# A four-layer decoder step on eight cores: tile-contiguous buffers, chained first loads, cast loads in order of use, and pooling by one 144-column band matmul

## The reference, cut to what matters

```python
def pool_mixer(h, buf, start_pos, w_pool, scale):      # layers 1 and 3, windows 2, 4, 8, 16
    ...
    p = (mean - hc[:, L:]).astype(h.dtype).reshape(B, T, N_POOL_GROUPS, GD_B)
    y = jnp.einsum('btgc,gce->btge', p, w_pool).reshape(B, T, D)
    return y * scale, hc[:, -L:].astype(h.dtype)

def trunk(x, ...):
    for i in range(DEPTH):
        h = rmsnorm(x, norm_mix[i])
        y = gmlp_mixer(h, ...) if i % 2 == 0 else pool_mixer(h, ...)
        x = x + y
        h = rmsnorm(x, norm_ffn[i])
        y, cb = conv_ffn(h, ...)          # silu(conv(h @ w_gate)) * (h @ w_val) @ w_down
        x = x + y
    return rmsnorm(x, norm_final), ...
```

## Time and profile before

| | us |
|---|---|
| median of 3 runs | 2949.17 (2947.11 to 3199.98) |
| the profiled execution | 2947.15 |
| its span (core 3; the cores lie between 2922.9 and 2945.6) | 2945.6 |

### The profile page before, as it was taken

The page is one execution under the profiler, slowest core; times in us unless marked ns, Lnnn a source line. Parts: engine busy times, 40 slices in busy tenths (PEclk is TensorE's granted clock), DMA queues, the critical chain, the costliest instruction groups (busy, mean ns, idle before and its releaser), DMA issues.

```text
span 2945.6 us, 52581 instructions; the slowest of 8 cores (2922.9 to 2945.6 us)
## 1 busy us (share of the span) xinstructions
PE 2812.8 (95%) x18576; PEld 1778.1 (60%) x18576; DVE 1489.3 (51%) x3134; ACT 1235.1 (42%) x2385; POOL 469.8 (16%) x832
## 2 busy tenths in 40 slices
PE   1999999999999999999987999999999999999998
PEld 0545666666654666666654566665766566666665
DVE  1266662565217566266531556626642366625753
ACT  1543443544244344354325434436433435435531
POOL 1002221132200222213220020020011020010001
PEclk9999999899999999999998999998999999998999
DMA  9516341554253543135444453322544335314421
GB/s 171 109 31 115 59 78 29 95 94 86 48 95 53 101 73 71 37 78 97 88 97 101 74 109 72 73 37 51 91 90 72 72 71 97 62 32 85 85 54 58
DMA packets 55425, 227.84 MB, mean 77 GB/s; under 512 B 6240, under 2 KB 25312, under 8 KB 37600
## 3 DMA queue, kind: packets, MB, share of 16 engines
q0 software_dynamic: 32960, 193.75, 37.4%
q1 hardware_dynamic: 22208, 30.72, 3.3%
HBM read 406.32 MB, written 13.32 MB: 142 GB/s over the span
## 4 chain that ended last, share of the span: by engine, by line
PE 87%; DMA 4%; DVE 3%; issue 3%; ACT 2%; DVEq 0%; SPq 0%; ACTq 0%
PE psum L720 27%; PE psum L989 22%; PE psum L982 21%; PE psum L786 8%; PE psum L809 4%; DMA xT<-x_in 4%; PE psum L945 2%; PE psum L649 1%; PE psum L897 1%; DVE vn_47 L823 1%; DVE vn_48 L823 0%; PE psum L841 0%; DVE nwt L743 0%; DMA gmlp_v<-gout 0%; DVE nwt L744 0%
## 5 line engine op out<-in xcount | busy, mean ns | idle before, releaser
L723 DVE TENSOR_TENSOR xT<-psum,xT 128x384 f32<-128x384 f32 (+2 forms) x288 | 148.0, 522 | 497.7 <-PE psum L720 482.2
L1006 DVE SCALAR_TENSOR_TENSOR cb_96<-psum,pvf,cb_96 128x384 f32<-128x384 f32 (+1 forms) x264 | 150.8, 571 | 70.3 <-ACT cb_96 L996 57.8
L1006 DVE SCALAR_TENSOR_TENSOR cb_97<-psum,pvf,cb_97 128x384 f32<-128x384 f32 (+1 forms) x264 | 150.7, 571 | 51.1 <-ACT cb_97 L996 31.0
L1006 DVE SCALAR_TENSOR_TENSOR cb_99<-psum,pvf,cb_99 128x384 f32<-128x384 f32 (+1 forms) x264 | 150.7, 571 | 48.9 <-ACT cb_99 L996 26.7
L1006 DVE SCALAR_TENSOR_TENSOR cb_98<-psum,pvf,cb_98 128x384 f32<-128x384 f32 (+1 forms) x264 | 150.6, 571 | 46.2 <-ACT cb_98 L996 32.9
L621 ACT ACTIVATE sq_59<-xT 128x384 f32<-128x384 f32 (+2 forms) x126 | 61.8, 491 | 191.0 <-DVE xT L723 174.0
L621 ACT ACTIVATE sq_60<-xT 128x384 f32<-128x384 f32 (+2 forms) x126 | 61.8, 491 | 171.7 <-DVE xT L723 155.6
L727 ACT ACTIVATE hB<-xT,pvd 128x384 bf16<-128x384 f32 (+1 forms) x96 | 55.4, 577 | 186.7 <-DVE xT L723 168.3
L996 ACT ACTIVATE cb_99<-psum,pvf 128x384 f32<-128x384 f32 (+2 forms) x132 | 84.4, 639 | 104.0 <-PE psum L982 103.8
L996 ACT ACTIVATE cb_96<-psum,pvf 128x384 f32<-128x384 f32 (+2 forms) x132 | 84.5, 640 | 99.3 <-PE psum L982 97.4
L672 DVE SCALAR_TENSOR_TENSOR hB<-xT,pvd,rstd_66 128x384 bf16<-128x384 f32 (+2 forms) x192 | 101.5, 600 | 45.6 <-ACT rstd_66 L664 41.4
(11 more groups left out here) (818 smaller groups left out, 6395.9 us busy)
## 6 DMA issues: line engine op xcount, KB each, us to landing
xT<-x_in SPq DMA_DIRECT2D x8, 768.0 KB, 19.8
y_out<-mT SPq DMA_DIRECT2D x8, 768.0 KB, 4.6
ASb<-st_conv SPq DMA_DIRECT2D x4, 1056.0 KB, 9.3
gvb<-g_v SPq DMA_DIRECT2D x4, 1024.0 KB, 8.2
pool_old<-st_old SPq DMA_DIRECT2D x2, 704.0 KB, 6.7
conv_sample<-cst SPq DMA_DIRECT2D x4, 352.0 KB, 6.3
xT<-x_in SPq DMA_DIRECT2D x2, 640.0 KB, 7.2
y_out<-mT SPq DMA_DIRECT2D x2, 640.0 KB, 6.3
```

Source lines behind the costliest of these rows:

```text
L723: rec(DVE, lambda e: e.tensor_tensor(out=xT.t[:, dc, c0:c0 + n], in0=pap(bk, 0, n), in1=xT.t[:, dc, c0:c0 + n], op=ALU.add), pt=[(bk, Fals ...
L1006: rec(DVE, lambda e: e.scalar_tensor_tensor(out=cb.t[:, 0:npr], in0=pap(gb, 2 - sh, 2 - sh + npr), scalar=sc(3 * l + 2 - sh), in1=cb.t[:, ...
```

## The change

- x, `mT` and `UB` get one buffer per tile, [128, blocks, n], so that a tile's rows follow each other without a gap in each partition; the z tiles, `vn` and `hS` move into parts of these buffers, and the final output has its own view of `mT` with whole rows.
- First loads: `pvd` first, then x tile 0; `Uu` 0 in two halves behind the first half of x tile 0; x tile 1 behind the first half of `Uu` 0; `Uu` 1 in two halves behind tile 1's first half; x tile 2 behind the first half of `Uu` 1; `Uu` 2 behind tile 2's first half. The very first u unit of tile 0 runs block of 128 input channels by block, over four PSUM banks, so that it can begin with the first normalised block. The Ln table is loaded by a small activation ahead.
- Each DMA of SP and POOL is ordered behind the one recorded before it in the same queue (`order`, for the planner alone, with no semaphore wait). The planner adds 0.5 us to the start of an operation that would change the ACT table when it compares candidates.
- Pooling: `band` gets 144 columns per group; one matmul over all 128 partitions writes a chunk's 128 columns and the first 16 of the next chunk. The chunk before a tile gives its 16 columns in one matmul of its own over 128 partitions. `bprev` is gone. Only the first matmul of a bank has `start`.
- Seam: `first_norm` of the next group's tile 0 comes after tile 1's load, those of tiles 1 and 2 after tile 2's load; its squares are added on DVE. The last tile of the run sums squares on PE, and its store goes in four parts.

```diff
@@ rec, schedule, emit
+        for o in order:
+            deps.setdefault(o, None)
...
-                if bs is None or s < bs - 1e-9:
+                k = s if op.tab is None or op.tab == lasttab[name] else s + 0.5
+                if bs is None or k < bk - 1e-9:
...
+                if u.deps[op] is None:
+                    u.ready = max(u.ready, op.start + op.cost)
...
@@ buffers
-        xT = alloc("xT", [128, KC, NTMAX], F32, pieces=grid(KC, NTMAX))
+        xv = {(g, t): alloc(f"xT{g}{t}", [128, KC, TILES[g][t][1]], F32, off=XO + sum(NT[:t]) * KC * 4, ...
...
+                mv[(g, t)] = alloc(f"mT{g}{t}", [128, FC, n], BF16, off=MO[t], ...
+                ubv[(g, t)] = alloc(f"UB{g}{t}", [128, EC, n], BF16, off=MO[t], ...
+                yv[(g, t)] = alloc(f"yT{g}{t}", [128, KC, n], F32, off=MO[t], ...
...
+        zb = [zalloc(f"z{c}", MO[0] + 6144 + 2048 * c) for c in range(3)]
+        zb += [zalloc(f"z{c}", MO[1] + o) for c, o in ((3, 0), (4, 2048), (5, 6144), (6, 8192), (7, 10240))]
...
@@ dma
+            op = rec(eng, lambda e: e.dma_start(out=out, in_=in_), reads, writes, cost, dsem, nbytes, behind=behind, order=fifo[eng.name][-1:])
+            fifo[eng.name].append(op)
...
@@ first loads
+        const_load(pvd, pvd.t[:, :, :].rearrange("p a b -> p (a b)"), vec_d, SP)
         xl0 = load_x(0, 0)
-        load_unit(("Uu", 0, 0, 0), behind=xl0[:1])
-        xl1 = load_x(0, 1, behind=xl0[1:])
-        load_unit(("Uu", 0, 0, 1))
-        xl2 = load_x(0, 2, behind=xl1[1:])
-        load_unit(("Uu", 0, 0, 2))
-        load_unit(("Uu", 0, 0, 3))
+        u0 = load_unit(("Uu", 0, 0, 0), behind=xl0[:1], parts=2)
+        xl1 = load_x(0, 1, behind=[u0.op0])
+        u1 = load_unit(("Uu", 0, 0, 1), behind=xl1[:1], parts=2)
+        xl2 = load_x(0, 2, behind=[u1.op0])
+        u2 = load_unit(("Uu", 0, 0, 2), behind=xl2[:1])
+        u3 = load_unit(("Uu", 0, 0, 3))
...
+        rec(ACT, lambda e: e.activation(out=rstd[1].t[:, 0:1], in_=epsb.t[:, 0:1], func=AF.Ln), ...
...
@@ mixer_a, first u unit of tile 0
+                    if (g, l, u, t) == (0, 0, 0, 0):
+                        b4 = palloc(4)
+                        for kc in range(KC):
+                            def mmu4(e):
+                                for e4 in range(4):
+                                    i = e.matmul(pap(b4, e4 * 512, e4 * 512 + n), lhsT=ub.t[:, kc, e4 * 128:(e4 + 1) * 128], ...
...
@@ mixer_b_tile
-                        else:
+                        if c == cl[0] and not (g == 0 and c == 0):
                             zp = zprev if c == 0 else ztile[c - 1]
-                            lst.append(((oc, oc + 128), zt.t[:, zh, es_], band.t[:, gi, :], True))
-                            lst.append(((oc, oc + 16), zp.t[96:128, zh, es_], bprev.t[96:128, gi, :], False))
+                            lst.append(((0, 16), zp.t[:, zh, es_], band.t[:, gi, 128:144]))
+                        tail = 0 if c == cl[-1] else 16
+                        if g == 0 and c == 0:
+                            lst.append(((0, 128), zt.t[:, zh, es_], bhi.t[:, gi, :]))
+                            lst.append(((0, 128), zt.t[:, zh, es_], blo.t[:, gi, :]))
+                            lst.append(((128, 144), zt.t[:, zh, es_], band.t[:, gi, 128:144]))
+                        else:
+                            lst.append(((oc, oc + 128 + tail), zt.t[:, zh, es_], band.t[:, gi, 0:128 + tail]))
...
@@ first_norm, final_tile, after_ffn
+                if lead:
+                    stat_add_pe(g, t, kc, DVE if kc % 2 else ACT)
+                else:
+                    stat_add(g, t, kc, DVE)
...
+            np_ = 4 if g == NG - 1 and t == 2 else 2
...
                             load_x(g + 1, t)
-                            first_norm(g + 1, t)
+                            if t > 0:
+                                first_norm(g + 1, t - 1)
+                            if t == 2:
+                                first_norm(g + 1, t)
```

More of the change, by code:

```diff
@@ L121, in __init__, with rec @@
         self.ops = []
-    def rec(self, eng, fn, reads=(), writes=(), cost=0.0, dsem=None, nbytes=0, tab=None, pt=(), behind=()):
+    def rec(self, eng, fn, reads=(), writes=(), cost=0.0, dsem=None, nbytes=0, tab=None, pt=(), behind=(), order=()):
         op = Op()
@@ L558, in build_program, with load_unit @@
         loaded = {}
-        def load_unit(key, behind=()):
+        def load_unit(key, behind=(), parts=1):
             i = unit_index[key]
             _, src, a, b, off, nb = units[i]
-            buf = alloc(f"w{i}", [128, a, b], BF16, off=R0 + off)
+            buf = alloc(f"w{i}", [128, a, b], BF16, off=R0 + off, pieces=[(h, h * a * b // parts, (h + 1) * a * b // parts) for h in range(parts)])
             so = src_off[src]
             sap = wts[so:so + 128 * a * b].rearrange("(p c) -> p c", p=128)
-            dma(POOL, buf.t[:, :, :].rearrange("p a b -> p (a b)"), sap, writes=buf.all, dsem=ring_sems[i % NRS], nbytes=128 * a * b * 4, behind=behind)
+            for h in range(parts):
+                cs_ = slice(h * a * b // parts, (h + 1) * a * b // parts)
+                buf.op = dma(POOL, buf.t[:, :, :].rearrange("p a b -> p (a b)")[:, cs_], sap[:, cs_], writes=[buf.r[h]], dsem=ring_sems[(i + 8 * h) % NRS],
+                             nbytes=128 * a * b * 4 // parts, behind=behind)
+                buf.op0 = buf.op0 if h else buf.op
+                behind = ()
             loaded[key] = buf
@@ L636, in stat_add @@
             d = a if kc < KC - 1 else accb[t % 2]
-            eng = POOL if kc < KC - 1 else DVE
+            eng = aeng or (POOL if kc < KC - 1 else DVE)
             rec(eng, lambda e: e.tensor_tensor(out=d.t[:, 0:n], in0=a.t[:, 0:n], in1=s.t[:, 0:n], op=ALU.add),
@@ L757, in mixer_a @@
             if first:
-                const_load(maskT, maskT.t[:], c_mask, behind=xl2[1:])
-            dma(SP, gvb.t[:], g_v[j].partition_broadcast(128), writes=gvb.all, dsem=gv_sem, nbytes=1048576, behind=xl2[1:] if first else ())
+                const_load(maskT, maskT.t[:], c_mask)
+            dma(SP, gvb.t[:], g_v[j].partition_broadcast(128), writes=gvb.all, dsem=gv_sem, nbytes=1048576, behind=[u3.op] if first else ())
             dma(POOL, wsT.t[:, :, :].rearrange("p a b -> p (a b)"), w_sT[j], writes=wsT.all, dsem=ws_sems[0], nbytes=524288)
@@ L1031, in mm_list @@
                 c0, n = TILES[g][t]
-                return ([(w.t[:, fc, :], mT.t[:, fc, c0:c0 + n]) for fc in range(FC)], w.all + [mT.r[(fc, t)] for fc in range(FC)])
+                return ([(w.t[:, fc, :], mv[(g, t)].t[:, fc, :]) for fc in range(FC)], w.all + [mv[(g, t)].r[fc] for fc in range(FC)])
             for t in range(3):
-                proj_tile(g, t, mm_list, l + 1 if l % 2 == 0 else None)
+                proj_tile(g, t, mm_list, l + 1 if l % 2 == 0 else None, l == DEPTH - 1)
                 after_tile(t)
         def first_norm(g, t):
+            lead = (g, t) == (0, 0)
             for kc in range(KC):
-                stat_add_pe(g, t, kc, DVE if (g == 0 and kc % 2) else ACT)
-            stat_finish(g, t, pe=True)
+                if lead:
+                    stat_add_pe(g, t, kc, DVE if kc % 2 else ACT)
+                else:
+                    stat_add(g, t, kc, DVE)
+            stat_finish(g, t, pe=lead)
             norm_tile(g, t, 0)
@@ L1169, in make_in_maps @@
     f = lambda k: np.asarray(inputs[k], dtype=np.float32)
-    mask, band, bhi, blo, bprev, bsmp = _consts()
+    mask, band, bhi, blo, bsmp = _consts()
     vd = np.concatenate([f("norm_mix"), f("norm_ffn"), f("norm_final").reshape(1, D), f("scale_b"), np.zeros((1, D), np.float32)], 0)
@@ L1185, in make_in_maps @@
         "w_sT": wsT, "w_sm": wsm.reshape(2, 64, 512), "b_big": np.ascontiguousarray(b_big), "b_smp": b_smp,
-        "c_mask": mask, "c_band": band, "c_bhi": bhi, "c_blo": blo, "c_bprev": bprev, "c_bsmp": bsmp,
+        "c_mask": mask, "c_band": band, "c_bhi": bhi, "c_blo": blo, "c_bsmp": bsmp,
     }
```

180 lines of the change are left out of this document (95 added, 85 removed).

## The result

The kernel after takes 2827.3 us (2825.5 to 2827.3), and 0.9591 of the time before, 95% interval 0.9569 to 0.9613. In some executions the cores of one die or of both run at a lower granted clock and take some per cent longer; all times and ratios here leave these out. Differences in us are against this 2827.3. The forecast of 2828 came out within 1 us. Its terms did not: two were too large, one too small, and they cancelled.

What follows compares the result with a forecast made beforehand. The prediction took PE's stream of matmuls as the bound. Gains of 46 (head), 47 (pooling), 25 (seam) and 1.5 (tail) sum to 119.5 us, giving 2828 us, with an 8-in-10 range of 2793 to 2874.

Steps and rivals of the forecast that it cites:

- Head: Start of the kernel: x and u units land earlier, v's first matmul at 84 instead of 129.95 us, gain 46.
- rival 4: DMA queues: a load that waits holds later ones, PE waits at 16 sub-layers, up to 3020 us; chance 0.03.
- Pooling: Four pooling stretches: 45 us from cheaper band pairs, 6 lost to new waits, 8 gained from the clock; gain 47.
- the sign of 5: Pooling: PE waiting for ACT or DVE for more than 5 us a stretch would show the prediction wrong.
- ACT is not the bound: 0: Whole kernel: fewer table changes save ACT time, but ACT is not the bound, so gain 0.
- Seam: Between the two groups: longer transfer rows, a sum by one matmul and earlier u work of tile 0; gain 25.
- Tail: End of the kernel: last sum off POOL and DVE, last store a quarter, less 0.5 for 8 matmuls; gain 1.5.
- 1: Pooling becomes bound by DVE and ACT and gives 12 us instead of 47: 2863 us; chance 0.15.
- 2: Head and seam: load chains are slow and the seam stays DMA-bound, gains 30 and 8: 2861 us; chance 0.13.
- 3: All gains plus full clock without new waits in pooling, and a head at 80: 2800 us; chance 0.17.
- Rival 5: Pooling: the band matmul stays at 0.15 us because of the write into the same bank, 2848 us; chance 0.07.
- The rule of the Trainium skill: Pooling: by the issue-gap formula a pair costs 81 ns and the change saves 1 us, 2872 us; chance 0.02.

Runs made afterwards that it cites:

- b_one: The kernel after, with the four bias rows loaded by one DMA and the two bias rows of the samples by another: 2822.1 us, ratio 0.9570.
- p_two_full: The kernel after, with each pooling pair as two matmuls of 128 and 16 columns, both over all 128 partitions: 2826.7 us, ratio 0.9585.
- the two pair runs: The kernel after, with each pooling pair as two matmuls, the second over all 128 partitions (2826.7 us) or over the last 32 as before (2875.3 us).

## Why the prediction was right in its sum and wrong in its terms

- **What bounds the kernel**: right. Idle PE time, wasted PE time and low clock were the three places, and all three gave.
- **Head, 46 forecast, 36.1 measured.** PE started at 16.6 for 15.5, steady u at 33.0 for 30, u ended at 89.8 for 84: each near, 6 late in the end, with waits for u units of 3.5 and 3.2. The step that failed is "the v units need 4.2 MB more ... about 80, in time". They landed until 98, and PE waited 4.9 for the last, because the four bias loads, counted there as "small constants", each waited for a landing and held the queue. That is rival 4's mechanism at one place; b_one takes 7.4 us of it back. "PE waiting for a weight unit anywhere" was one of the signs of being wrong, and it came. The reason given for the gain, that nothing competes with x's tile 0, was half right: the order of the loads keeps competitors away (without it the head is 26 us longer, 30.5 in the mean), the new links on top of it are worth 3 to 6. "Loads in order of use: 0" was thus wrong in the other direction.
- **Pooling, 47 forecast, 66.5 measured.** The 45 for the pairs held, and p_two_full confirmed its reason. The two corrections were both too small and cancelled: clock 14 for 8 (a remainder), new waits 13 for 6. The reason for the waits was off, too: in the first stretch PE waits 1.8 us for ACT's evictions of z (L937), and 0.7 for DVE's residual adds (L988). With 3.6 to 5.3 us of idle PE a stretch, two of the four are just above the sign of 5. What was missing is the ACT table: "ACT is not the bound: 0" should have been 13 to 18. The busy share hid it; ACT's queue order, with an eviction behind three table loads, shows it in the trace of before. With pairs and table loads both back, the pooling is as long as before, so no part of it stays open.
- **Seam, 25 forecast, 15.5 measured.** Both causes were right, 7.6 for the rows and 5.9 for the order with the place of the sums. The size failed at "I expect 8 us of wait to stay" (11.9 stayed, since x stood behind the stores in its queue) and at the u part, taken as 54 and measured 60.7 without its waits: the lower clock after each wait, which the head's sum had counted and this one had not, is part of that.
- **Tail**: 1.4 for 1.5 (from the last `Wd` mark to the end 88.2 before, 86.8 after).
- **Rivals.** 1 and 2 came true in part (13 us of new waits; head and seam both short), 3 in part (the clock). Rival 5 is out: over all partitions the second write costs nothing. The rule of the Trainium skill (TensorE: Matmul & The Clock Gate, Back-to-back issue gap) is out, too: by it the pairs would cost 19 us (240 x 0.081) and bring 1, and they brought 46. The same section of the Trainium skill gives this formula for a matmul by itself and has about 81 ns for one of 128 columns in a stream with weight loads, which the prediction left out. Neither comes to the 0.26 us of a pair, and the 0.06 us between full-partition matmuls here are nearer the formula. The Trainium skill's TensorEngine Tiling (Array Packing), Key Properties, on the drain at a change of the tiling mode, agrees with the two pair runs, which show its price and not the drain itself.

The sum was right because -10 and -9.5 met +19.5, and that is luck: with head and seam read rightly and the pooling left at 47, it would have been about 2847.

## What to carry to other kernels

An engine far from its limit can still hold the one that bounds: look at what stands in its queue behind a table load or a DMA that waits, and who waits for that. Links between loads pay only together with an order of the queue, and small loads that wait for each other belong in one DMA or at the end. A small matmul over fewer partitions costs its step there and back, not its columns; the same matmul over all partitions is nearly free.
